# A hybrid encoder layer on one Trainium2 core: the input read with its channels first, the token's scale applied to the products

## The chip, the cores and the metric

The kernel runs on one core of a Trainium2 chip. The metric is the device time of one execution in microseconds (us). The engines are TensorE (PE in the profile; PEld is its weight load), VectorE (DVE), ScalarE (ACT), GpSimd (POOL) and SyncE (SP), which here issues nearly all DMA. Each engine works through its own instructions in order; semaphores tie the engines together.

## The reference, cut to what matters

One layer over two independent sequences (512 and 1024 tokens, laid behind each other: 1536 tokens, 1024 channels, all float32):

```python
u = x * rsqrt(mean(x*x, -1) + EPS) * g_norm            # EPS = 1e-6
z = u @ w_in                                           # 1024 -> 3072 columns
q, k, v, g_att, xr, g_lru = split(z, 512 columns each)
o_att = diff_attention(rms_norm(q), rms_norm(k), v)    # q, k normed per 32 columns
o_lru = rg_lru(conv4(xr))   # gates sigmoid(y @ w), two recurrences (forward, backward)
h = x + concat(o_att * silu(g_att), o_lru * silu(g_lru)) @ w_out
y = h + rms_norm((p @ w_ple) * sigmoid(h @ w_pg)) * g_ple
```

The change touches `u`, `z` and what takes `z` out of PSUM.

## The kernel before

**Arithmetic.** Every large product is done in three matmuls: each operand is split into a high part (fp32r) and the rest (`hi`, `lo`), and PE adds hi\*hi, lo\*hi and hi\*lo. ACT makes each `hi` by a copy, DVE or POOL makes each `lo` by a subtraction.

**The start (tokens to `u`).** For each of 12 tiles of 128 tokens: SP loads the tile `x_sb` (`load_x`, L470), ACT sums its squares (`square_x`, L1017), POOL makes the scale 1/sqrt (`x_scale`: L844, then a power, L846), DVE multiplies by scale and gain (`normalise`, L1349), PE turns it in 8 transposes (`transpose_u`, L1731), ACT splits off `u_hi` from PSUM (`split_u`, L1022) and DVE makes `u_lo` (`u_low`, L1354). The gain `g_norm` is spread over the partitions by 8 transposes first (L1773, L1341).

**The z blocks.** The 12 blocks of 128 columns of xr, g_lru and g_att (`m` = 0 to 11) times 3 blocks of 512 tokens (`b`) are 36 z blocks. The list `ZB` gives their order; a block's place in it is its number i, from 0. `z_block(i)` is 24 matmuls (L1721 to L1723) into one of three PSUM banks `b_ps[i % 3]`, so block i waits until block i - 3 has left PSUM (`z_evac`). The weights of a block come from `load_wA` (L475), `wA_high` (ACT, L1029) and `wA_low` (POOL, L854).
An xr block leaves PSUM by a DVE copy into XP (L1364). A gate block leaves it in two steps: `z_sigmoid` on ACT (L1059, PSUM to `z_stage`), then a DVE product of it with the PSUM bank (L1368), which frees the bank; SP stores it (`store_z`). The blocks of tiles 4 to 11 are turned between the matmuls of z blocks 0 to 3.

**The recurrence among the z blocks.** A loop over c = 0, 1, 2 does nine z blocks each, from number r = 9c + 8, and among them one group of 128 recurrence channels (channel group 3 follows among the q, k and v products). On PE: the six small gate products `gate(6c)` to `gate(6c+5)`, `gates = {0: (0, 1), 1: (2,), 3: (3, 4), 4: (5,)}`: gates 0 and 1 ahead of block r, 2 ahead of r+1, 3 and 4 ahead of r+3, 5 ahead of r+4 (numbers modulo 6). Gate g waits for `sig_done` g - 1, the ACT sigmoids of gates 0 to g - 2. Gate 6c waits for the convolution's result Y (`conv_taps`, DVE) and for its copy with swapped halves (`swap_rows`, a DMA). On ACT and DVE, in the order of the code (a part):

```python
# ACT                               # DVE
z_sigmoid(r)                        z_out_of_psum(r)
sig(g + 2)                          z_out_of_psum(r + 1)
z_sigmoid(r + 1)                    root_argument(c, 0)   # L1447
decays(c, 0)  # L1071, 1074, 1077   scan(c, 0)            # L1455, L1461
root(c, 0)    # L1081               z_out_of_psum(r + 2), (r + 3), (r + 4)
z_sigmoid(r + 2)                    conv_taps(c + 1, (0, 1, 2))
sig(g + 3)    # L1047, L1048        root_argument(c, 1)
```

**After it.** 36 products of q, k and v by tokens (L1817 to L1819), then 96 attention steps and the output products.

Of the kernel before, what the change touches and what calls it, by code (L numbers as in the profile page):

```python
# [30 lines left out]
P = 128  # L31
# [39 lines left out]
def encoder_layer(nc, x, p_in, g_norm, w_in, norms, lams, rel_bias, onehot, chan, w_a, w_x,  # L71
# [19 lines left out]
    with ctx:  # L91
# [11 lines left out]
        chan_sb = sb("chan_sb", [P, LC, 11])  # L103
        rate = sb("rate", [P, LC, 2])
# [3 lines left out]
        sums = sb("sums", [P, 5, 2])  # L108
        rsum = sb("rsum", [P, 24, 2])
# [3 lines left out]
        u_hi = sb("u_hi", [P, KC, T], F32R, phase1)  # L113
        u_lo = sb("u_lo", [P, KC, T], F32R, phase1)
        z_stage = sb("z_stage", [P, NB, 512], F32, phase1)
        sq_junk = z_stage
        wB_hi = [sb("wB_hi", [P, KC, 512], F32R, phase1)]
# [10 lines left out]
        wA_hi = sb("wA_hi", [P, 3, KC, P], F32R, phase1)  # L128
# [4 lines left out]
        ssq = sb("ssq", [P, 2, 16], F32, phase1)  # L133
        msq = sb("msq", [P, 2, 16], F32, phase1)
        rsq = sb("rsq", [P, 2, 16], F32, phase1)
        ph1a = ExitStack()
        x_sb = sb("x_sb", [P, 4, D], F32, ph1a)
        u_tok = sb("u_tok", [P, 2, D], F32, ph1a)
        gnB = sb("gnB", [P, D], F32, ph1a)
        x_junk = sb("x_junk", [P, D], F32, ph1a)  # L140
        ssx = sb("ssx", [P, 4], F32, ph1a)
        msx = sb("msx", [P, 4], F32, ph1a)
        rsx = sb("rsx", [P, 4], F32, ph1a)
# [91 lines left out]
        def k_tile(u, hh):  # L235
# [62 lines left out]
        const_in = sem("const_in"); gnB_in = sem("gnB_in"); gn_turned = sem("gn_turned"); soft_step = sem("soft_step")  # L298
# [4 lines left out]
        x_sq = sem("x_sq"); x_ms = sem("x_ms"); x_rs = sem("x_rs"); u_done = sem("u_done")  # L303
        uT_done = sem("uT_done"); uhi_done = sem("uhi_done"); ulo_done = sem("ulo_done")
# [35 lines left out]
            "g_in", "mixed", "hp_in0", "hp_in1", "x_sum", "m_hi", "m_lo", "p_in", "p_hi", "p_lo", "x_in", "gp_in",  # L340
# [43 lines left out]
        def uT_slot(n):  # L384
            if n == 2:
                return b_ps[:, 1:3, :].rearrange("p a b -> p (a b)")
            return (uT_ps[:, 0:2, :].rearrange("p a b -> p (a b)") if n == 0 or n % 2 and n > 1 else
                    qT_ps[:].rearrange("p a b c -> p (a b c)"))

        ZB = [(0, 0), (1, 0), (0, 1), (1, 1), (0, 2), (2, 0), (1, 2), (2, 1), (2, 2)]  # L390
        ZB += [(m, b) for m in range(3, 3 * LC) for b in range(NB)]
        LASTM = 3 * (LC - 1) + 1
        XR = (0, 2, 5, 8)

        def z_row(m):
            return m + 1 if m == LASTM + 1 else m
# [64 lines left out]
        def _(sp):  # L461
# [5 lines left out]
            def load_x(n):  # L467
                if n >= 4:
                    sp.wait_ge(u_done, n - 3)
                sp.dma_start(x_sb[:, n % 4, :], x[n * P:(n + 1) * P, :]).then_inc(x_in[n % 4], 16)  # L470

            def load_wA(m):
                if m >= 3:
                    sp.wait_ge(z_mm, z_blocks_to(m - 3))
                sp.dma_start(wA_raw[:, m % 3, :, :],  # L475
                             w_in.rearrange("(k p) c -> p k c", p=P)[:, :, 3 * A + m * P:3 * A + (m + 1) * P]
                             ).then_inc(wA_in[m % 3], 16)

            load_x(0)
            load_x(1)  # L480
            load_x(2)
            load_x(3)
            load_wA(0)
            load_x(4)
            load_x(5)
            load_wA(1)
            load_x(6)
            load_x(7)
# [7 lines left out]
            load_x(8)  # L496
            load_x(9)
            load_wA(2)
            load_x(10)
            load_x(11)  # L500

            def store_z(i):
# [4 lines left out]
                sp.wait_ge(z_evac, i + 1)  # L507
# [18 lines left out]
            def load_gate(c):  # L526
                if c:
                    sp.wait_ge(lru_out, 64 * c)
                for slot, stored in z_stored(gate_row(c)):
                    sp.wait_ge(z_out[slot], stored)  # L530
                row = z_row(gate_row(c)) * P
                sp.dma_start(G_[:, 0:LONG], z_ch[row:row + P, TOK0:T]).then_inc(lru_g_in, 16)
                sp.dma_start(G_[:, YS:YS + SHORT], z_ch[row:row + P, 0:TOK0]).then_inc(lru_g_in, 16)
# [15 lines left out]
            store_z(0)  # L549
            store_z(1)  # L550
            store_z(2)
            store_z(3)
            load_wA(3)
            store_z(4)
            sp.wait_ge(lru_clear, 1)
            load_gate_w(0)
            sp.wait_ge(line_sb, 4)
            sp.dma_start(line_d, line_st[:]).then_inc(line_out, 16)
            swap_rows(0)
            store_z(6)  # L560
            load_wA(4)
            store_z(7)
# [229 lines left out]
            for k in range(PC):  # L792
# [7 lines left out]
                         ).then_inc(fin["gp_in"], 16)  # L800
# [33 lines left out]
        def _(gp):  # L834
# [13 lines left out]
            def x_scale(n):  # L848
                rsqrt(n, ssx[:, n % 4:n % 4 + 1], msx[:, n % 4:n % 4 + 1], rsx[:, n % 4:n % 4 + 1], 1, D,
                      x_sq, x_ms, x_rs)  # L850

            def wA_low(m):
                gp.wait_ge(wAhi_done, m + 1)
                gp.tensor_tensor(wA_lo[:, m % 3, :, :], wA_raw[:, m % 3, :, :], wA_hi[:, m % 3, :, :].bitcast(F32),  # L854
# [14 lines left out]
            for n in range(NT):  # L869
                x_scale(n)  # L870
                if n == 3:
                    wA_low(0)
                if n == 5:
                    wA_low(1)
                if n == 11:
                    wA_low(2)
# [15 lines left out]
            step(gp.tensor_scalar(spv[2], spv[1], 1.0 / 17, 1.0 / 15, ALU.mult, ALU.add))  # L892
# [1180 lines left out]
```

## Time and profile before

| | us |
|---|---|
| median of 3 runs (1056.28 to 1058.12) | 1057.22 |
| the profiled execution | 1057.25 |
| its span | 1055.4 |
| PE busy | 1015.6 (96%) |
| DVE busy | 650.1 (62%) |
| ACT busy | 579.8 (55%) |
| POOL busy | 517.9 (49%) |

1.85 us of the profiled execution lie outside its span. PE is busy in nearly all of it; of 40 slices of 26.4 us the first is the one in which PE is busy for half only.

### The profile page before, as it was taken

The numbers are of one execution on the slowest core, as the hardware profiler recorded it, in microseconds if no ns is written. First come the engines' busy times: TensorE is split into PE (matmuls) and PEld (weight loads), VectorE is DVE, ScalarE is ACT, GpSimd is POOL, SyncE is SP. The second block draws the span as 40 slices with busy tenths as digits, with TensorE's granted clock in tenths as the row PEclk, the third lists the DMA queues.
The fourth block names the chain that finished last, engine by engine and source line by source line (L and its number), as shares of the span: only waits on it lengthen the run. The fifth ranks groups of instructions, "written<-read, shape, count | busy, mean of one in ns | idle before, by whom it ended". The sixth has DMA issues, their size and how long they took to land.

```text
span 1055.4 us, 15541 instructions
## 1 busy us (share of the span) xinstructions
PE 1015.6 (96%) x5856; PEld 806.3 (76%) x5856; DVE 650.1 (62%) x1026; ACT 579.8 (55%) x879; POOL 517.9 (49%) x421
## 2 busy tenths in 40 slices
PE   5999999999999999988999999999999999999997
PEld 4777877677787888866777777777778888888885
DVE  6743636574576251149999999999966355445423
ACT  6536567583653131159999999999962212112112
POOL 5252234526467542016666776766668143444421
PEclk8999999999999999999999999999999999999999
DMA  7231634323254624929876577364185222432221
GB/s 239 84 99 60 204 120 125 121 77 127 61 160 140 179 80 140 284 94 227 206 178 171 147 178 205 94 163 136 53 298 186 82 91 85 131 124 85 96 89 40
DMA packets 114810, 144.06 MB, mean 136 GB/s; under 512 B 10024, under 2 KB 80808, under 8 KB 114728
## 3 DMA queue, kind: packets, MB, share of 16 engines
q1 hardware_dynamic: 114592, 143.06, 45.6%
q8 instruction: 47, 0.77, 0.3%
q14 instruction: 27, 0.22, 0.1%
q10 hardware_dynamic: 144, 0.00, 0.0%
HBM read 95.78 MB, written 44.11 MB: 133 GB/s over the span
## 4 chain that ended last, share of the span: by engine, by line
PE 67%; DVE 18%; issue 10%; ACT 4%; DMA 1%; POOL 0%; DVEq 0%; POOLq 0%; SPq 0%; ACTq 0%
DVE E_ L1545 11%; PE b_ps L1721 5%; PE b_ps L1722 5%; PE b_ps L1723 5%; PE b_ps L1817 5%; PE b_ps L1819 5%; PE b_ps L1818 5%; PE g_ps L1721 4%; PE g_ps L1723 4%; PE g_ps L1722 4%; PE o_ps L1878 3%; PE w_ps L1861 2%; PE h_ps L1721 2%; PE h_ps L1723 2%; PE h_ps L1722 2%
## 5 line engine op out<-in xcount | busy, mean ns | idle before, releaser
L1188 ACT ACTIVATE E_<-E_,nmax 128x1024 f32<-128x1024 f32 (+1 forms) x184 | 186.7, 1017 | 15.0 <-DVE nmax L1545 14.7
L1545 DVE CUSTOM_DVE_ANT_0 E_<-s_ps,bias 128x1024 f32<-128x1024 f32 (+1 forms) x184 | 188.0, 1056 | 3.6 <-PE s_ps L1830 3.6
L930 POOL TENSOR_TENSOR E_<-E_,ratio 128x576 f32<-128x576 f32 (+3 forms) x92 | 84.7, 920 | 85.5 <-DVE E_ L1561 85.5
L1721 PE MATMUL b_ps<-u_hi,wA_hi 128*128 128x512 f32 x288 | 115.5, 401 | 5.3 <-DVE u_lo L1354 4.9
L1722 PE MATMUL b_ps<-u_lo,wA_hi 128*128 128x512 f32 x288 | 113.0, 392 | 0.0
L1723 PE MATMUL b_ps<-u_hi,wA_lo 128*128 128x512 f32 x288 | 112.9, 392 | 0.0
L933 POOL TENSOR_TENSOR E_<-E_ 128x576 f32<-128x576 f32 (+3 forms) x92 | 103.8, 1128 | 7.2
L1830 PE MATMUL s_ps<-KL,QL 128*128 128x512 f32 x256 | 90.3, 434 | 14.0 <-DVE nmax L1545 13.2
L1861 PE MATMUL w_ps<-ident,E_ 128*128 128x128 f32 x624 | 83.5, 273 | 1.8 <-ACT WT L1216 1.7
L1216 ACT ACTIVATE WT<-w_ps 128x1024 f32<-128x1024 f32 (+1 forms) x96 | 83.4, 868 | 2.8 <-PE w_ps L1861 2.6
L1878 PE MATMUL o_ps<-WT,V 128*64 128x128 f32 x1280 | 84.0, 278 | 0.0
L1861 PEld LDWEIGHTS w_ps<-ident,E_ 128*128 128x128 f32 x624 | 72.6, 141 | 14.8 <-issue 3.9
L1878 PEld LDWEIGHTS o_ps<-WT,V 128*64 128x64 f32 x1280 | 68.6, 136 | 18.8 <-issue 18.8
L1817 PE MATMUL b_ps<-wB_hi,u_hi 128*128 128x512 f32 x192 | 76.0, 396 | 0.5 <-DVE z_stage L1368 0.5
L1721 PEld LDWEIGHTS b_ps<-u_hi,wA_hi 128*128 128x128 f32 x288 | 54.4, 189 | 28.4 <-issue 17.7
L1721 PE MATMUL g_ps<-wg_hi,h_hi 128*128 128x512 f32 x192 | 75.6, 394 | 0.0
L1819 PE MATMUL b_ps<-wB_hi,u_lo 128*128 128x512 f32 x192 | 74.9, 390 | 0.0
L1723 PE MATMUL g_ps<-wg_hi,h_lo 128*128 128x512 f32 x192 | 74.8, 390 | 0.0
L1722 PE MATMUL g_ps<-wg_lo,h_hi 128*128 128x512 f32 x192 | 74.8, 389 | 0.0
L1818 PE MATMUL b_ps<-wB_lo,u_hi 128*128 128x512 f32 x192 | 74.7, 389 | 0.0
L854 POOL TENSOR_TENSOR wA_lo<-wA_raw,wA_hi 128x1024 fp32r<-128x1024 f32 x12 | 30.1, 2504 | 88.8 <-ACT wA_hi L1029 88.6
L846 POOL TENSOR_TENSOR rsq<-msq,neghalf 128x16 f32<-128x16 f32 x24 | 70.5, 2939 | 2.0
(226 smaller groups left out, 2338.5 us busy)
## 6 DMA issues: line engine op xcount, KB each, us to landing
QL<-qk_t SPq DMA_DIRECT2D x32, 256.0 KB, 6.3
KL<-qk_t SPq DMA_DIRECT2D x32, 256.0 KB, 7.7
bias<-line_d SPq DMA_DIRECT2D x8, 960.0 KB, 11.2
x_sb<-in_x SPq DMA_DIRECT2D x12, 512.0 KB, 5.0
wA_raw<-in_w_in SPq DMA_DIRECT2D x12, 512.0 KB, 4.1
z_ch<-z_stage SPq DMA_DIRECT2D x24, 256.0 KB, 2.0
qk_t<-qh SPq DMA_DIRECT2D x24, 256.0 KB, 2.3
qk_t<-ql SPq DMA_DIRECT2D x24, 256.0 KB, 2.8
```

The costliest lines, as they stand in the source:

```text
L933: gp.tensor_tensor(one, one, two, ALU.add).then_inc(w_gp, 1)
L1188: act.activation(e, e, ACT.Exp, bias=nmax[:, n % 5, c:c + 1], scale=-1.0, accum_out=sums[:, n % 5, c:c + 1]).then_inc(e_done, 1)
L1545: dve.tensor_tensor_reduce(weights_at(n)[:, c, 0:n_tok], s_ps[:, c, 0:n_tok], b[:, ::-1], -1.0, 3e38, ALU.add, ALU.min, nmax[:, n % 5, c:c ...
L1721: pe.matmul(dst, sh, mh, start=k == 0, stop=False)
L1722: pe.matmul(dst, sh, ml, start=False, stop=False)
L1723: mm = pe.matmul(dst, sl, mh, start=False, stop=k == n - 1)
L1817: pe.matmul(dst, u_hi[:, k, c], wB_hi[g][:, k, :], start=k == 0, stop=False)
L1818: pe.matmul(dst, u_hi[:, k, c], wB_lo[g][:, k, :], start=False, stop=False)
L1819: mm = pe.matmul(dst, u_lo[:, k, c], wB_hi[g][:, k, :], start=False, stop=k == KC - 1)
L1830: mm = pe.matmul(s_ps[:, c, b * 512:(b + 1) * 512], q_tile(u, hh)[:, c, qt * P:(qt + 1) * P], k_tile(u, hh)[:, c, b * 512:(b + 1) * 512], ...
L1861: mm = pe.transpose(w_ps[:, k, :], weights_at(n)[:, 0, k * P:(k + 1) * P], ident[:])
L1878: mm = pe.matmul(o_ps[HV * j:HV * j + HV, 0, pair * P:(pair + 1) * P], V_at[i % 2][:, first // P + k, HV * (head % 2):HV * (head % 2) + HV ...
```

## The change

The host passes the tokens a second time with the channels first (`x_t`), and the columns of the z blocks as 12 contiguous blocks (`w_cols`). `u` is now x times the gain only: ACT makes `u_hi` from the loaded `u_raw` with the gain as its scale, DVE makes `u_lo`; nothing is transposed for it. The scale of a token is still made from `x_sb`, four tiles at a time; PE spreads it over the partitions (`spread_row`, four transposes for 512 tokens), DVE copies it into `row`, and DVE multiplies each z block by it on its way out of PSUM (`z_scale`). The sigmoid of a gate block then reads the scaled `z_stage` and writes the PSUM bank `z_gate()`, and a second DVE product (`z_gated`) makes the result. q and k go unscaled (their own norm removes the factor; its EPS is scaled by `epsx`), v is scaled by the ACT copy that takes it out of PSUM. ZB, the loop's order (`LATE`) and the buffers of the weights change with it.

```diff
-        ZB = [(0, 0), (1, 0), (0, 1), (1, 1), (0, 2), (2, 0), (1, 2), (2, 1), (2, 2)]
+        ZB = [(0, 0), (1, 0), (2, 0), (0, 1), (1, 1), (0, 2), (2, 1), (1, 2), (2, 2)]
-        XR = (0, 2, 5, 8)
+        XR = (0, 3, 5, 8)
+        LATE = (2, 1, 0)
 # SP
+            load_xT(0, 0)
+            sp.dma_start(wA_raw[:, 0, 0:KC // 2, :], w_cols[0, :, 0:KC // 2, :]).then_inc(wA_half_in, 16)
+            sp.dma_start(wA_raw[:, 0, KC // 2:KC, :], w_cols[0, :, KC // 2:KC, :]).then_inc(wA_in[0], 16)
+            load_xT(0, 1)
             load_wA(1)
+            load_xT(0, 2)
+            load_xT(0, 3)
+            load_wA(2)
+            for n in range(4):
+                load_x(n)
+            sp.wait_ge(uhi_done, KC)
+            for j in range(KC // 2):
+                load_xT(1, j)
 # POOL
+            wA_low(0)
+            wA_low(1)
+            wA_low(2)
+            for b in range(NB):
+                x_scale(b)
 # ACT
+                act.activation(u_hi[:, b, k, :], u_raw[:, b, k, :], ACT.Copy, scale=g_col[:, k:k + 1]
+                               ).then_inc(uhi_done, 1)
...
+            wA_high(2)
             for n in range(4):
                 square_x(n)
+            for k in range(KC):
+                u_high(1, k)
+            z_sigmoid(1)
+            z_sigmoid(2)
+            for n in range(4, 8):
+                square_x(n)
+            for k in range(KC):
+                u_high(2, k)
+            z_sigmoid(4)
+            for n in range(8, NT):
+                square_x(n)
...
             def z_sigmoid(i):
-                act.wait_ge(z_mm, i + 1)
-                act.activation(z_stage[:, n % NB, :], b_ps[:, i % NB, :], ACT.Sigmoid).then_inc(z_sig, 1)
+                act.wait_ge(z_evac, i + 1)
+                act.wait_ge(z_fin, n)
+                act.activation(z_gate(), z_stage[:, n % NB, :], ACT.Sigmoid).then_inc(z_sig, 1)
...
+                def z_sigmoids(first, last):
+                    for i in range(first, min(last, 9)):
+                        z_sigmoid(r + i)
+                        if i == 3:
+                            wA_high(3 * c + 5)
+                        if i == 6 and c < LC - 2:
+                            wA_high(3 * c + 6)
...
-                z_sigmoid(r + 1)
+                z_sigmoids(late + 1, late + 2)
                 decays(c, 0)
                 root(c, 0)
-                z_sigmoid(r + 2)
+                z_sigmoids(late + 2, late + 3)
                 sig(g + 3)
 # DVE
+                dve.scalar_tensor_tensor(out=u_lo[:, b, k, :], in0=u_raw[:, b, k, :], scalar=g_col[:, k:k + 1],
+                                         in1=u_hi[:, b, k, :].bitcast(F32), op0=ALU.mult, op1=ALU.subtract
+                                         ).then_inc(ulo_done, 1)
...
+                    dve.tensor_tensor(z_stage[:, n % NB, :], b_ps[:, i % NB, :], tokens, ALU.mult
                                       ).then_inc(z_evac, 1)
+            def z_gated(i):
+                dve.wait_ge(z_sig, z_sigs(i))
+                dve.tensor_tensor(z_stage[:, n % NB, :], z_stage[:, n % NB, :], z_gate(), ALU.mult).then_inc(z_fin, 1)
+            def z_out_of_psum(i):
+                z_scale(i)
+                z_gated(i - 1)
...
+            row_out(0)
+            z_scale(0)
+            z_scale(1)
+            for k in range(KC):
+                u_low(1, k)
+            z_gated(1)
+            z_scale(2)
+            z_gated(2)
...
+                z_blocks(0, late + 2)
                 root_argument(c, 0)
                 scan(c, 0)
-                for i in range(2, 5):
-                    z_out_of_psum(r + i)
+                z_blocks(late + 2, late + 5)
 # PE
+            keep_busy(12)
+            z_block(0)
+            z_block(1)
+            z_block(2, lambda k: spread_row(0) if k == 4 else None)
+            z_block(3)
+            z_block(4, lambda k: spread_row(1) if k == 5 else None)
+            z_block(5)
+            z_block(6, lambda k: spread_row(2) if k == 5 else None)
+            z_block(7)
...
+                gates = {late: (0, 1), late + 1: (2,), late + 3: (3, 4), late + 4: (5,)}
```

`keep_busy(12)` is 12 transposes of the identity. `z_blocks(a, b)` is `z_out_of_psum` for r + a to r + b - 1. `spread_row(b)` waits for the scales of block b, which need the squares of its four tiles. Where a list says `LATE[c]`, all of channel group c's steps sit `late` blocks later among the z blocks than before.

## Rows read from the trace of the kernel before

**Rows 1.** Page, parts 1 and 2, busy time and slices:

```profile
PE 1015.6 (96%) x5856; PEld 806.3 (76%) x5856; DVE 650.1 (62%) x1026; ACT 579.8 (55%) x879; POOL 517.9 (49%) x421
PE   5999999999999999988999999999999999999997
```

**Rows 2.** Windows; after each engine's name its busy us, then granted clock, DMA share, GB/s:

```profile
0.00:20.00 20.00, 9.09 (x41) 7.31 (x42) 11.29 (x10) 14.44 (x20) 11.15 (x21) 0.93 0.85 278
75.00:252.00 177.00, 176.48 (x843) 130.31 (x841) 96.55 (x73) 115.25 (x122) 68.78 (x21) 1.00 0.35 110
```

**Rows 3.** Timeline of PE, start: start, duration, instruction, idle before it and releaser:

```profile
19.85 0.77 PE L1721 MATMUL b_ps<-u_hi,wA_hi 128*128 128x512 f32 x1 [4.32 <-DVE u_lo L1354]
20.84 0.63 PE L1723 MATMUL b_ps<-u_hi,wA_lo 128*128 128x512 f32 x1
21.27 0.63 PE L1721 MATMUL b_ps<-u_hi,wA_hi 128*128 128x512 f32 x1
```

**Rows 4.** Windows of the start, columns as in Rows 2:

```profile
6.00:7.00 1.00, 0.00 (x0) 0.00 (x0) 0.24 (x1) 1.00 (x2) 0.56 (x1) 1.00 1.06 434
7.00:8.00 1.00, 0.00 (x0) 0.00 (x0) 1.00 (x1) 0.82 (x2) 0.87 (x1) 1.00 0.96 380
20.00:22.00 2.00, 2.00 (x5) 1.62 (x6) 2.00 (x1) 0.43 (x2) 1.92 (x2) 0.50 0.09 26
```

**Rows 5.** Timeline of ACT: the first square, and a split:

```profile
4.57 1.06 ACT L1017 ACTIVATE x_junk<-x_sb 128x1024 f32<-128x1024 f32 x1 [2.09 <-DMA x_sb<-in_x]
5.89 1.06 ACT L1017 ACTIVATE x_junk<-x_sb 128x1024 f32<-128x1024 f32 x1 [0.17 <-DMA x_sb<-in_x]
13.03 1.05 ACT L1029 ACTIVATE wA_hi<-wA_raw 128x1024 fp32r<-128x1024 f32 x1
```

**Rows 6.** Timeline of DVE and of POOL between 14 and 24 us:

```profile
14.29 1.22 DVE L1354 TENSOR_TENSOR u_lo<-qT_ps,u_hi 128x1024 fp32r<-128x1024 f32 x1
19.62 4.50 DVE L1349 SCALAR_TENSOR_TENSOR u_tok<-x_sb,rsx,gnB 128x1024 f32<-128x1024 f32 x2
14.15 2.45 POOL L854 TENSOR_TENSOR wA_lo<-wA_raw,wA_hi 128x1024 fp32r<-128x1024 f32 x1 [1.42 <-ACT wA_hi L1029]
19.47 2.37 POOL L854 TENSOR_TENSOR wA_lo<-wA_raw,wA_hi 128x1024 fp32r<-128x1024 f32 x1 [1.01 <-ACT wA_hi L1029]
```

**Rows 7.** Timeline of PE in loop c = 0: gates 0, 3, 5 and the starts of blocks 9, 11:

```profile
75.50 0.64 PE L1765 MATMUL uT_ps<-Y,gate_w 64*64 64x512 f32 x1
84.06 0.50 PE L1721 MATMUL b_ps<-u_hi,wA_hi 128*128 128x512 f32 x1
95.19 0.64 PE L1765 MATMUL uT_ps<-Y,gate_w 64*64 64x512 f32 x1
97.07 0.50 PE L1721 MATMUL b_ps<-u_hi,wA_hi 128*128 128x512 f32 x1
102.84 0.64 PE L1765 MATMUL uT_ps<-Y,gate_w 64*64 64x512 f32 x1
```

**Rows 8.** Timeline of ACT and of DVE in loop c = 0:

```profile
89.86 0.60 ACT L1059 ACTIVATE z_stage<-b_ps 128x512 f32<-128x512 f32 x1 [4.39 <-PE b_ps L1723]
98.23 1.49 ACT L1081 ACTIVATE TH<-TH 128x1539 f32<-128x1539 f32 x1 [0.53 <-DVE TH L1447]
101.04 0.60 ACT L1059 ACTIVATE z_stage<-b_ps 128x512 f32<-128x512 f32 x1
102.10 0.69 ACT L1048 ACTIVATE I_<-qT_ps,chan_sb 128x512 f32<-128x512 f32 x1
104.84 1.27 DVE L1368 TENSOR_TENSOR z_stage<-z_stage,b_ps 128x512 f32<-128x512 f32 x2
```

**Rows 9.** Timeline of DVE and of SP around the swap of c = 1, and the copy's DMA line:

```profile
117.95 1.82 DVE L1431 SCALAR_TENSOR_TENSOR Y<-XP,chan_sb,Y 128x1539 f32<-128x1539 f32 x1
120.84 1.14 SPq L524 DMA_DIRECT2D Ysw<-Y  x2
Ysw<-Y SPq DMA_DIRECT2D x8, 384.8 KB, 4.4
```

## What the change was predicted to do

> **What bounds the kernel now.** I read the page's first two parts first. PE is busy for 96% of the span, and the slices show one weak place, the first, where it is half idle [rows 1]. The windows sharpen this: 9.1 of the first 20.0 us, but 176.5 of the 177.0 us between 75 and 252 us [rows 2]. So PE bounds the z blocks, and time is to be had ahead of them. The timeline of PE shows how: the first z matmul starts at 19.85 us, after an idle of 4.32 us [rows 3].
>
> A busy bound is not the only one. The timeline of loop c = 0 shows block 11 starting at 97.07 and gate 5 at 102.84 [rows 7]: 5.77 us for a block. Two blocks from 84.06 to 95.19 take 11.13 us [rows 7], so I count 5.46 a block (and 0.1 or 0.2 where a gate follows). Gate 5 starts just as ACT ends what it waits for: the sigmoid L1048 runs from 102.10 to 102.79 [rows 8]. So a second chain (sigmoid of block 9, decays, root, sigmoid of block 10, `sig(3)`, gate 5) runs beside PE with no slack. That is where a later hand-over shows.
>
> **The start.** Block 8 and the gates ahead of it come at 75.50 us before [rows 7]; I work out the same point after.
> - Landing. The first 512 KB tile is there at 4.57 us [rows 5], and then 434 and 380 GB/s flow [rows 4], about 1.3 us for 512 KB. In SP's new order the pieces of block 0 land at 4.6, 7.2, 9.8 and 11.1, the halves of the first weights at 5.2 and 5.9, wA 1 and 2 at 8.5 and 12.4, the four x tiles from 13.7 to 17.6.
> - The splits. A 1024-column copy on ACT takes 1.05 [rows 5], so 512 columns 0.55; a DVE operation on 512 columns 0.65 (two in 1.27 [rows 8]). `u_high(0, 0)` 4.6 to 5.2, `u_low` 5.8, the first `wA_lo` half 6.5: the first z matmul at 6.6, 13.3 us earlier than before [rows 3].
> - The lock. `u_low` took its input from PSUM and ran in 1.22 us beside POOL's `wA_lo` [rows 6]. Now it reads two SBUF operands, as `normalise` does, and two of those at 19.62 took 4.50 us together where POOL held `wA_lo` from 19.47 to 21.84 [rows 6]; free of it they would take about 2.4, as `u_low` twice. So such an operation waits POOL's whole 2.4 us. `wA_low(1)` (9.7 to 12.1) holds up `u_low(0, 4)`, `wA_low(2)` (13.9 to 16.3) holds up `u_low(0, 7)`. Block 0 then ends at 17.65, without the lock at 13.5. I take 17.65, and keep 4.1 us as the bound.
> - Blocks 1 and 2 to 29.1 with `spread_row`. `u_low(1, k)` stands behind `row_out(0)` and two `z_scale`, and goes on in step with PE (0.65 each against 0.69 for three matmuls): block 3 from 29.1 to 34.7.
> - Block 4 stops at its k = 5, 38.1, for `spread_row(1)`. That needs the squares of tiles 4 to 7, which stand on ACT behind `z_sigmoid(2)`, thus behind `z_scale(2)`, thus behind all of `u_low(1, k)`: 33.4, `z_gated(1)` 34.0, `z_scale(2)` 34.6, the sigmoid 35.3, four squares at 1.32 each (4.57 to 5.89 [rows 5]) 40.6, POOL's scale 42.1. A stop of 4.0 us; block 4 ends at 44.65, block 5 at 50.1.
> - Block 6 stops likewise at its k = 5 for tiles 8 to 11, whose squares stand behind `z_sigmoid(4)`: 53.5 to 55.4. It ends at 57.9, block 7 at 63.4, `lines` at 64.4.
>
> Block 8 is reached at 64.4 instead of 75.5: 11.1 us saved. With the lock's 4.1 back, 15.2 at most; with a slow PE after the stops, 9.
>
> A rule of the Trainium skill bears on this (SBUF — State Buffer, "SBUF: two separate sides"): a DVE operation with two SBUF inputs and a GpSimd one take the pair of ports as an exclusive lock for a whole instruction. The page names no such lock for an operation with one PSUM input. The trace agrees with both halves [rows 6]. Taken away, the rule would put my sum at 4.1 us less; by the 358 GB/s that the Trainium skill gives for a core's HBM reads (DMA: Bandwidth & Descriptors, "Specifications") block 0 would land 0.9 us later. Against that figure stand 434 and 380 GB/s here [rows 4], and the measurement decides.
>
> **The loops c = 0 to 2.** I count from the end of block r + late + 1, the last whose sigmoid stands ahead of `decays(c, 0)`. Before, that is block 9, whose sigmoid starts at 89.86; the root ends at 99.72, DVE's scan at 104.84, ACT's next sigmoid starts at 101.04, gate 5 at 102.84 [rows 8, 7].
> - In front of the sigmoid now stand `z_scale` (0.7) and, in c = 1, `z_gated(18)` (0.6), since `z_sigmoid` waits for both.
> - After the root `z_sigmoid(r + late + 2)` no longer reads PSUM. It waits for `z_scale` of the same block, which stands on DVE behind the scan, until 104.84 on the old scale instead of 101.04, then 0.65 for the scale and 0.6 for a `z_gated`. The sigmoid starts 5.1 us later; `sig(g + 3)` is queued behind it, and gate 5 of the group, and with it PE, behind that.
> - In c = 1 the step i = 3 falls there too, and `wA_high(8)` (0.95) goes in front of `sig(9)`.
> - Sums. c = 1: 0.7 + 0.6 + 5.1 + 1.0 = 7.4 us. c = 2 (block 26 is xr, the weight step lies behind): 0.7 + 5.1 = 5.8. c = 0: blocks 9 to 11 are xr, so `decays` starts right after `sig(2)`, which gives back nearly all: 0.6.
>
> Together 13.8 us of new stops of PE, where before there was none to speak of. Bounds: 11 (if DVE's small steps overlap better) and 16.
> - The copy for gate 6 and 12. Y was done at 119.77, its swap issued by 121.98 and landed 4.4 later [rows 9], five us before PE came. The blocks between `decays(c, 1)` and that gate fall from four to three, 5.46 less, and `z_scale`, `z_gated` and `wA_high(6)` lengthen the way: 1.5 and 1.6 us of stop, 3.1 together (0 to 5).
> - The clock. After 4.32 us idle PE ran at half rate: start to start 0.43 us [rows 3], clock 0.50 [rows 4], against 0.23 later (5.46 over 24); nine matmuls so before it rose, 1.8 us. The stops of 7.4 and 5.8 are longer than that idle: 3.6 us, 0 to 5.4 with the one of 4.0 at the start.
> - 24 more DVE products of 0.69 beside 96.6 busy of 177 [rows 2] cost nothing as work; without that room they would be 16 us. ACT and POOL do no more than before. Attention and the output are the same code, and PE is on their path, so the shift reaches the end.
>
> **Sum**, against the profiled execution (1057.25; span 1055.4 and 1.85 around it; the median is 1057.22): 1057.25 - 11.1 + 13.8 + 3.1 + 3.6 = 1066.65. I say 1066.5.
>
> **Rivals.**
> 1. Faster: the hand-over through `z_scale` stays off the path, and the start pays. Mechanism: PE reaches the fifth gate late enough, or DVE gets the scale out before the scan. Then only 0.7 three times is added: 1057.25 - 11.1 + 2.1 = 1048, and 1044 without the lock. It decides where the new stops of the loops stay under 11.1 us together. For it: DVE is half idle [rows 2]. Against: both queues are in order, and gate 5 had no slack [rows 7, 8].
> 2. Gains and losses cancel: lock gone (-15.2), stops at their lower bound (11 + 2), clock kept: 1055 to 1059.
> 3. The start gains nothing, as its loads have doubled and all stops run at the low clock: 1057.25 - 7 + 16 + 5 + 5.4 = 1077.
> 4. The change doesn't do what it says: the scale's own chain (x tiles, squares, spread) is still ahead of the first blocks' exit, so that z would wait as before: the stops of 4.0 and 1.9 us are this, and no more, unless the banks fill earlier.
>
> **Numbers.** The forecast's case has 0.60, with its own range 1061 to 1073; rival 1 has 0.27, rival 2 0.08 (half of it within 0.2%, a quarter to each side), rival 3 (with 4) 0.05. About 0.2%, 2 us, is what a measurement can tell from no change. Faster 0.29, same 0.04, slower 0.67. The range for 8 in 10 takes in the upper part of rival 1: 1048 to 1073.
>
> **What would show it.** First z matmul near 6.6 us. PE idle of about 4 us inside block 4. POOL's `wA_lo` beside a stretched `u_lo`. The gates ahead of block 8's neighbours: block 8 starting near 64. Idle of 7 and 6 us ahead of the sixth gate in c = 1 and c = 2, ended by the ACT sigmoid, the ACT queue waiting for DVE's `z_scale` after the scan, and clock 0.50 after them. Wrong it would be if PE runs densely from 64 us on: then the time is near 1048.

## The result, and the profile after

| | before | after |
|---|---|---|
| median (4 runs each, on one chip) | 1057.53 (1056.28 to 1058.12) | 1083.4 (1082.54 to 1085.43) |
| the profiled execution | 1057.25 | 1083.45 |
| its span | 1055.4 | 1081.6 |
| PE's granted clock, mean over the span | 0.995 | 0.983 |

The changed kernel is slower: after / before = 1.0249, with a 95% interval of 1.0231 to 1.0267. The forecast was 1066.5 with a range of 1048 to 1073. So the direction was right, the time lies 10 us above the range, and 16.9 us of the size are missing.

The page after, parts 1 and 2 (busy time and slices), answers to [rows 1]:

```profile
PE 1015.1 (94%) x5776; PEld 801.7 (74%) x5776; DVE 653.8 (60%) x1053; ACT 583.1 (54%) x891; POOL 511.7 (47%) x406
PE   6899988779999999997999999999999999999997
PEclk9999998889999999999999999999999999999999
```

PE's busy time is as before, though it does 80 matmuls less. The first slice is a little better, 6 for 5, the second a little worse, 8 for 9. Then slices 6 to 9 (27.0 us each, so 135 to 243 us) show 8, 8, 7, 7 where before there were nines, and from slice 7 to 9 the granted clock falls. Two windows, answering to [rows 2], put numbers on it:

```profile
0.00:20.00 20.00, 11.48 (x39) 8.66 (x39) 10.71 (x9) 13.96 (x20) 7.40 (x10) 1.00 0.90 334
75.00:252.00 177.00, 151.84 (x690) 109.23 (x689) 86.47 (x72) 97.16 (x102) 58.94 (x18) 0.92 0.30 97
```

Between 75 and 252 us PE did 690 matmuls where it had done 843, at a mean clock of 0.92. All other engines did less in it too: nobody was overloaded, all of them waited. So the loss is one of order, and the timeline of PE names each wait. Here are the start and the idle times up to gate 20 (two of the start's small ones left out); start, duration, instruction, in brackets the idle before it and its releaser. It answers to [rows 3, 7]:

```profile
8.83 0.77 PE L1805 MATMUL b_ps<-u_hi,wA_hi 128*128 128x512 f32 x1 [4.45 <-DVE wA_lo L1450]
18.04 0.50 PE L1805 MATMUL b_ps<-u_hi,wA_hi 128*128 128x512 f32 x1 [1.83 <-DVE u_lo L1410]
43.72 0.94 PE L1813 MATMUL uT_ps<-ident,rsx 128*128 128x128 f32 x4 [3.42 <-POOL rsx L888]
66.16 0.50 PE L1805 MATMUL b_ps<-u_hi,wA_first_hi 128*128 128x512 f32 x1
105.10 0.64 PE L1859 MATMUL uT_ps<-Y,gate_w 64*64 64x512 f32 x1 [0.53 <-ACT I_ L1094]
130.26 0.61 PE L1859 MATMUL uT_ps<-Y,gate_w 64*64 64x512 f32 x1 [2.08 <-DMA Ysw<-Y]
166.40 1.11 PE L1859 MATMUL uT_ps<-Y,gate_w 64*64 64x512 f32 x1 [8.82 <-ACT I_ L1094]
194.00 0.96 PE L1859 MATMUL uT_ps<-Y,gate_w 64*64 64x512 f32 x1 [2.72 <-DMA Ysw<-Y]
207.07 0.64 PE L1859 MATMUL uT_ps<-Y,gate_w 64*64 64x512 f32 x1 [3.78 <-ACT I_ L1094]
235.62 1.11 PE L1859 MATMUL uT_ps<-Y,gate_w 64*64 64x512 f32 x1 [7.23 <-ACT I_ L1094]
267.50 0.61 PE L1859 MATMUL uT_ps<-Y,gate_w 64*64 64x512 f32 x1 [0.40 <-DMA Ysw<-Y]
275.05 0.64 PE L1859 MATMUL uT_ps<-Y,gate_w 64*64 64x512 f32 x1
```

In order these are: the first z matmul; the last stop in block 0 (one of 0.69 us lies ahead of it); block 4 at its `spread_row(1)` (one of 0.19 us follows in block 6); block 8; then gates 5, 6, 11, 12, 14, 17, 18; and gate 20, which comes after the loops. The trace of before has gate 20 here:

```profile
250.52 0.64 PE L1765 MATMUL uT_ps<-Y,gate_w 64*64 64x512 f32 x1
```

**Where the 26.2 us of the span went.** I cut both traces at the same two places, gate 20 and block 8 (before with gates 0 and 1 ahead of it, which after stand ahead of block 10 and so behind this cut).
- Up to block 8: 66.16 for 75.50 [rows 7], -9.3.
- Block 8 to gate 20: 275.05 - 66.16 = 208.9, before 250.52 - 75.50 = 175.0: +33.9. The idle times of the fence between the two add up to 25.6, before they are some 0.3. What is left, 8.6, is slow running behind them: four windows below give 8.4 by the granted clock.
- Gate 20 to the end of the span: 806.55 for 804.88, +1.7. One idle time in the q products is 2.29 us here and 1.04 before, and behind it the clock was 0.50 from 354.6 to 358.0, which is 1.7 more; 1.2 us of these 3.0 come back ahead of the attention.

**The hand-over, hop by hop.** This is the sixth gate of c = 1 (gate 11, idle 8.82), on DVE:

```profile
144.63 0.69 DVE L1432 TENSOR_TENSOR z_stage<-b_ps,row 128x512 f32<-128x512 f32 x1 [6.01 <-PE b_ps L1807]
145.24 0.68 DVE L1441 TENSOR_TENSOR z_stage<-z_stage,qT_ps 128x512 f32<-128x512 f32 x1
157.71 3.36 DVE L1541 TENSOR_TENSOR_SCAN HF<-A_,I_ 128x1539 f32<-128x1539 f32 x1
160.99 0.67 DVE L1432 TENSOR_TENSOR z_stage<-b_ps,row 128x512 f32<-128x512 f32 x1
161.57 0.68 DVE L1441 TENSOR_TENSOR z_stage<-z_stage,qT_ps 128x512 f32<-128x512 f32 x1
```

and on ACT:

```profile
146.01 0.60 ACT L1104 ACTIVATE qT_ps<-z_stage 128x512 f32<-128x512 f32 x1 [5.54 <-DVE z_stage L1441]
154.38 1.49 ACT L1126 ACTIVATE TH<-TH 128x1539 f32<-128x1539 f32 x1 [0.53 <-DVE TH L1527]
162.32 1.28 ACT L1104 ACT_TABLE_LOAD   x1 [6.45 <-DVE z_stage L1441]
163.62 0.60 ACT L1104 ACTIVATE qT_ps<-z_stage 128x512 f32<-128x512 f32 x1
164.15 1.04 ACT L1075 ACTIVATE wA_hi<-wA_raw 128x1024 fp32r<-128x1024 f32 x1
165.67 0.68 ACT L1094 ACTIVATE I_<-qT_ps,chan_sb 128x512 f32<-128x512 f32 x1
```

Read it from the end. PE starts gate 11 at 166.40, when `sig(9)` (165.67) is done. In ACT's queue there stand ahead of it the copy `wA_high(8)`, the sigmoid of the next z block and the table load for it, and all that waits from 155.87 to 162.32. DVE has the product `z_gated` that releases it at 161.57 only, since `z_scale` of the same block (160.99) stands behind the scan (157.71, 3.36). The bank was full long before. Before the change the same sigmoid read PSUM itself and came 2.81 us after the start of the root [rows 8]; here it is 9.24 us.

One hop was not foreseen. Before, the table was loaded right behind the root: the root ended at 99.72 and the sigmoid ran at 101.04 [rows 8]. Here the load stands behind the wait for DVE, so its 1.28 us lie on the chain too. The load before:

```profile
99.74 1.28 ACT L1059 ACT_TABLE_LOAD   x1
```

### The profile page after: what moved, and what is told of

The parts are those of the page before. It is cut to its first block, busy times and chain, and to the rows that moved or that the text cites. A ratio compares the mean times of both kernels' runs of the same rounds, so it can differ in the third digit from the quotient of the medians.

```text
span 1081.6 us, 15433 instructions
## 1 busy us (share of the span) xinstructions
PE 1015.1 (94%) x5776; PEld 801.7 (74%) x5776; DVE 653.8 (60%) x1053; ACT 583.1 (54%) x891; POOL 511.7 (47%) x406
## 4 chain that ended last, share of the span: by engine, by line
PE 56%; DVE 22%; issue 12%; ACT 7%; DMA 2%; POOL 1%; SPq 0%; DVEq 0%; POOLq 0%; ACTq 0%
DVE E_ L1629 10%; PE b_ps L1908 5%; PE b_ps L1910 5%; PE b_ps L1909 5%; PE g_ps L1805 4%; PE g_ps L1807 4%; PE g_ps L1806 4%; PE b_ps L1805 3%; PE b_ps L1807 2%; PE o_ps L1971 2%; PE b_ps L1806 2%; PE w_ps L1954 2%; PE s_ps L1921 2%; PE h_ps L1805 2%; PE h_ps L1807 2%
## 5 line engine op out<-in xcount | busy, mean ns | idle before, releaser
L1805 PE MATMUL b_ps<-u_hi,wA_hi 128*128 128x512 f32 x240 | 99.0, 412 | 7.1 <-DVE wA_lo L1450 4.4
L1921 PE MATMUL s_ps<-KL,QL 128*128 128x512 f32 x256 | 90.8, 436 | 13.8 <-DVE nmax L1629 13.0
L1806 PE MATMUL b_ps<-u_lo,wA_hi 128*128 128x512 f32 x240 | 96.2, 401 | 0.0
L1954 PEld LDWEIGHTS w_ps<-ident,E_ 128*128 128x128 f32 x624 | 72.6, 140 | 14.9 <-issue 3.8
L896 POOL TENSOR_TENSOR wA_lo<-wA_raw,wA_hi 128x1024 fp32r<-128x1024 f32 (+1 forms) x10 | 26.9, 2694 | 91.5 <-ACT wA_hi L1075 91.5
L1805 PEld LDWEIGHTS b_ps<-u_hi,wA_hi 128*128 128x128 f32 x240 | 47.1, 196 | 29.9 <-issue 10.5
## 6 DMA issues: line engine op xcount, KB each, us to landing
bias<-line_d SPq DMA_DIRECT2D x8, 960.0 KB, 11.1
```

The source lines that it names most:

```text
L1805: pe.matmul(dst, sh, mh, start=k == 0, stop=False)
L1806: pe.matmul(dst, sh, ml, start=False, stop=False)
L1921: mm = pe.matmul(s_ps[:, c, b * 512:(b + 1) * 512], q_tile(u, hh)[:, c, qt * P:(qt + 1) * P], k_tile(u, hh)[:, c, b * 512:(b + 1) * 512], ...
L1954: mm = pe.transpose(w_ps[:, k, :], weights_at(n)[:, 0, k * P:(k + 1) * P], ident[:])
```

## Experiments

All times are medians; each ratio is against the kernel before, run on the same chip. All edits are made to the changed kernel, except where another is named. The last four columns are idle times of PE in us, ahead of the gate or in the block named.

| kernel | us | ratio (95% interval) | block 4 | gate 11 | gate 14 | gate 17 |
|---|---|---|---|---|---|---|
| after | 1083.4 | 1.0249 (1.0231 to 1.0267) | 3.42 | 8.82 | 3.78 | 7.23 |
| e1_scale_first | 1068.53 | 1.0114 (1.0099 to 1.0129) | 3.42 | 2.40 | 3.78 | 0.80 |
| e2_weights_behind_sig | 1079.38 | 1.0213 (1.0197 to 1.0228) | 3.42 | 8.82 | none | 7.23 |
| e3_squares_first | 1078.17 | 1.0203 (1.0188 to 1.0218) | none | 8.82 | 3.78 | 7.23 |
| e10_swap_first | 1081.27 | 1.0219 (1.0200 to 1.0239) | 3.46 | 8.82 | 3.78 | 7.23 |
| e7_lock_at_start | 1080.85 | 1.0228 (1.0214 to 1.0241) | 3.43 | 8.83 | 3.78 | 7.23 |
| e8_pe_kept_busy | 1083.32 | 1.0246 (1.0233 to 1.0260) | 3.47 | 2.27 | 3.78 | 0.67 |
| e4_all_four | 1058.51 | 1.0013 (1.0003 to 1.0022) | none | 2.40 | none | 4.43 |
| e5_table_early | 1057.64 | 1.0008 (0.9999 to 1.0017) | none | 2.40 | none | 4.43 |
| e6_root_and_sigs_early | 1049.43 | 0.9932 (0.9918 to 0.9945) | none | 0.93 | none | 0.66 |
| e9_best | 1048.09 | 0.9917 (0.9902 to 0.9932) | none | 0.93 | none | 0.62 |

The kernel before took 1056.9 to 1057.1 beside these runs. Executions of one of these kernels differ by up to 5.5 us (e6: 1047.50 to 1052.99). One thing that differs from trace to trace, at places where the code is the same, is where PE ran at clock 0.50 (the last section lists it). So gains of 2 us are read from the traces as well.

**e1: the scale of one block ahead of the scan.**

```diff
                 root_argument(c, 0)
+                z_blocks(late + 2, late + 3)
                 scan(c, 0)
-                z_blocks(late + 2, late + 5)
+                z_blocks(late + 3, late + 5)
```

> DVE does z_out_of_psum(r + late + 2) between root_argument(c, 0) and scan(c, 0) instead of behind the scan; nothing else differs from the changed kernel (1083.4 us). Theory (queue order): the ACT sigmoid, and with it sig(g + 3) and the sixth gate, waited for a product that DVE had room for 5.1 us earlier. Then the idle of PE ahead of the sixth gate falls from 8.8 to 3.7 us in c = 1 and from 7.2 to 2.1 in c = 2, the 0.5 in c = 0 goes, and with less low clock the time is 1067 to 1071. Rival (capacity): DVE or ACT has too much work in these stretches, so that the idle only moves; it stays above 6 us in both and the time above 1080.

1068.53, 14.9 us less than after. DVE's product is now at 156.93, the table load at 158.56 and the scan at 160.38; gate 11 waits 2.40 and gate 17 0.80:

```profile
157.05 1.49 ACT L1126 ACTIVATE TH<-TH 128x1539 f32<-128x1539 f32 x1 [0.53 <-DVE TH L1527]
156.93 0.68 DVE L1432 TENSOR_TENSOR z_stage<-b_ps,row 128x512 f32<-128x512 f32 x1
160.38 3.36 DVE L1541 TENSOR_TENSOR_SCAN HF<-A_,I_ 128x1539 f32<-128x1539 f32 x1
```

The scan was not put off by it: it starts 3.33 us behind the root (157.05, in after 154.38) in both, because DVE had stood idle there for 1.56 us, waiting for the root. The two waits fell 1.3 us lower than I expected (3.7 and 2.1), since the table load now runs right behind the root. This is the main cause, shown: one place in DVE's order. The idle removed is 13.4 us (0.53, 6.42, 6.43), and 1.0 comes back at gate 18 (1.41 for 0.40); the rest of the gain is less slow running, clock 0.96 for 0.92 between 75 and 252 us.

**e2: the weights' copy behind the group's first sigmoid.**

```diff
-                wA_high(3 * c + 4)
                 z_sigmoids(0, late)
                 sig(g)
+                wA_high(3 * c + 4)
                 sig(g + 1)
```

> ACT does wA_high(3c + 4) between sig(g) and sig(g + 1), as before the change, instead of ahead of sig(g). Theory: the 3.8 us idle ahead of gate 14 is a wait of this split for the last z block of its buffer (two buffers where there were three), with sig(12) queued behind it; it goes, with 1.7 us of low clock behind it: 1077 to 1079. Rival: gate 14 is late because the swapped copy came late and everything on ACT with it; then the idle stays over 3 us and the time at 1083.

1079.38, 4.0 us less (its executions: 1077.63 to 1081.06). Gate 14's 3.78 is gone, the other waits stand. On ACT after (the kernel as changed), the wait is this:

```profile
203.39 1.06 ACT L1075 ACTIVATE wA_hi<-wA_raw 128x1024 fp32r<-128x1024 f32 x1 [8.08 <-PE b_ps L1807]
204.46 1.28 ACT L1093 ACT_TABLE_LOAD   x1
206.34 0.68 ACT L1094 ACTIVATE I_<-uT_ps,chan_sb 128x512 f32<-128x512 f32 x1
```

`wA_high(10)` writes one of two buffers, which only the last matmul of block 26 frees. It waits 8.08 us for it, with the table load and `sig(12)` queued behind, and gate 14 waits for `sig(12)`. The copy itself isn't wanted for three blocks yet.

**e3: the squares ahead of the sigmoids.**

```diff
-            z_sigmoid(1)
-            z_sigmoid(2)
             for n in range(4, 8):
                 square_x(n)
+            z_sigmoid(1)
+            z_sigmoid(2)
             for k in range(KC):
                 u_high(2, k)
-            z_sigmoid(4)
             for n in range(8, NT):
                 square_x(n)
+            z_sigmoid(4)
```

> ACT does the squares of tiles 4 to 7 ahead of z_sigmoid(1) and z_sigmoid(2), and those of 8 to 11 ahead of z_sigmoid(4). Theory: the 3.4 us idle of PE inside block 4 is the scale's chain queued behind a sigmoid that waits for DVE; it goes, and 1.7 us of low clock behind it, and the shift reaches the end: 1078 (1077 to 1080). Rival (given back): the loops' stops are set by chains that do not start earlier when PE does, and take up the gain: 1082 to 1084.

1078.17, 5.2 us less, for a stop of 3.42. Behind the stop PE had run slowly, and now it doesn't. First after, then e3, the window behind block 4's stop (columns as in Rows 2; the number before the DMA share is the clock):

```profile
44.00:47.00 3.00, 3.00 (x10) 2.45 (x9) 2.96 (x6) 3.00 (x6) 0.43 (x1) 0.50 0.81 314
```

```profile
44.00:47.00 3.00, 3.00 (x15) 2.49 (x14) 3.00 (x5) 1.81 (x3) 0.00 (x0) 1.00 1.02 408
```

Ten matmuls in three microseconds against fifteen: some 1.7 us of the 5.2 fits this. It isn't a price of its own, though: e1's execution had the same stop of 3.42 with clock 1.00 behind it, and there block 6 waited 1.82 instead of 0.19, so that block 8 came equally far behind the stop (22.46 us for 22.44). What e3 takes away is the chain of the squares.

**e10: the swap ahead of a store in SP's queue.**

```diff
-                store_z(r + 5)
                 swap_rows(c + 1)
+                store_z(r + 5)
```

> The changed kernel (1083.4 us) with swap_rows(c + 1) issued ahead of store_z(r + 5), nothing else. Theory: in c = 1 SP waits for z_gated(22) ahead of the swap, 1.3 us behind the convolution's last tap; the idle ahead of gate 12 falls from 2.7 to about 1.3 us, that ahead of gate 6 stays near 2.1: 1081.5 to 1083. Rival: the idle is the DMA's own landing (4.4 us) and stays 2.7: 1083.4.

1081.27, 2.1 us less; the two intervals overlap a little, so the time alone doesn't show it. After (the kernel as changed), SP issued them so:

```profile
187.69 0.33 SPq L533 DMA_DIRECT2D z_ch<-z_stage  x1
188.11 1.15 SPq L549 DMA_DIRECT2D Ysw<-Y  x2
```

Y was done at 186.47 (184.65 and 1.82). The store ahead of the swap waited for its block's `z_gated`, which the change had put behind a `z_scale`. Before, the swap stood behind a store too, 1.07 us behind Y [rows 9]; here it is 1.64. With the swap first, gate 12 waits 0.95 instead of 2.72, and from gate 11 to gate 14 it takes 37.2 us for 40.7: the 1.8 of idle and 1.7 of slow running behind it. Against that, e10's execution had a slow stretch behind gate 6 that after's had not. Gate 6's own wait hardly changed (1.91 for 2.08): its swap had no wait ahead of it.

**e7: block 0's third `wA_lo` on DVE instead of POOL.**

```diff
 # POOL
-            wA_low(2)
 # DVE, behind u_low(0, 7)
+            dve.wait_ge(wAhi_done, 4)
+            dve.wait_ge(wAlo_done, 3)
+            dve.tensor_tensor(wA_lo[:, 2, :, :], wA_raw[:, 2, :, :], wA_high_at(2).bitcast(F32),
+                              ALU.subtract).then_inc(wAlo_done, 1)
```

> The changed kernel (1083.4 us) with wA_low(2) done by DVE behind u_low(0, 7) instead of by POOL beside it; POOL keeps wA_low(0) and wA_low(1). Theory (lock): the 1.8 us idle of PE in block 0 is u_low(0, 7) held up by POOL's wA_lo; it goes, and u_lo of 512 columns takes 0.75 us throughout the second half of block 0. Time 1081 to 1082. Rival (landing): k = 6 and 7 come late by DMA or by the ACT copies, and the idle stays above 1.2 us; time 1083.

1080.85, 2.5 us less, with intervals that just overlap. Block 0's last stop (1.83) is gone, and block 1 starts at 17.29 for 19.53. The same four `u_low` in after, with POOL's operation at that time, and then in e7:

```profile
12.11 6.54 DVE L1410 SCALAR_TENSOR_TENSOR u_lo<-u_raw,g_col,u_hi 128x512 fp32r<-128x512 f32 x4 [0.41 <-ACT u_hi L1062]
15.06 2.38 POOL L896 TENSOR_TENSOR wA_lo<-wA_raw,wA_first_hi 128x1024 fp32r<-128x1024 f32 x1 [1.11 <-ACT wA_first_hi L1075]
```

```profile
12.24 4.09 DVE L1409 SCALAR_TENSOR_TENSOR u_lo<-u_raw,g_col,u_hi 128x512 fp32r<-128x512 f32 x4 [0.70 <-ACT u_hi L1061]
```

The difference, 2.45, matches POOL's 2.38. So the rival, landing, is out for this stop.

**e8: PE kept busy through the waits.** In c = 1 and 2, 60 transposes of the identity ahead of the sixth gate; they write a z bank that is free.

```diff
                 for i in range(9):
+                    if c and i == late + 4:
+                        pe.wait_ge(z_evac, r + i - NB + 1)
+                        for _ in range(60):
+                            pe.transpose(b_ps[:, (r + i) % NB, 0:P], ident[:], ident[:])
```

> The changed kernel with 60 transposes of the identity on PE (into a PSUM bank about to be overwritten) ahead of the sixth gates of c = 1 and c = 2, 6.5 us of the idle 8.8 and 7.2. No wait is taken away. Theory: half rate behind these two stops costs half of the busy time at 0.50, (170.3 - 166.4)/2 + (242.0 - 235.6)/2 = 5.2 us; with PE busy the clock stays up and they come back: 1078 (1077 to 1079.5). Rival: the low clock is hidden, since the stops that follow are set by ACT and DVE chains and not by PE: 1082 to 1084.

1083.32, no different from after: the expected 5 us didn't come. What the clock does behind gate 17 is as expected, first in after, then in e8:

```profile
237.60:242.00 4.40, 4.40 (x12) 3.45 (x12) 0.00 (x0) 1.74 (x3) 3.74 (x2) 0.51 0.00 0
```

```profile
237.70:242.00 4.30, 4.30 (x23) 2.92 (x24) 0.00 (x0) 3.67 (x6) 1.70 (x1) 1.00 0.16 61
```

and gate 17 to gate 18 took 28.9 us for 31.9. But in c = 1 the filling fell short by 2.27 us, and the clock fell behind it all the same. And behind gate 6, where the edit does nothing, the clock was 1.00 in after's execution and 0.54 in this one, with nearly the same idle ahead of it (2.08 and 2.16). First after, then e8:

```profile
130.30:134.20 3.90, 3.90 (x25) 2.25 (x26) 3.83 (x3) 1.56 (x2) 0.44 (x1) 1.00 0.96 314
```

```profile
130.80:134.20 3.40, 3.40 (x16) 0.85 (x16) 3.33 (x3) 1.25 (x2) 0.13 (x1) 0.54 0.96 345
```

The places of the gates say where the expected 5.2 went. Gate 11 comes 2.2 us later than in after, 1.7 of it by the slow stretch behind gate 6. Behind gate 11 nearly as much ran slow as before. The 3.0 us behind gate 17 did come back: gate 18 is 0.9 us earlier than in after. So slow running does cost time on PE's path, and this run's equal time is, in the profiled execution, 3.0 us won against some 2 lost; what it was in the other executions isn't known.

**e4: edits 1, 2, 3 and 10 together.**

> The three edits together, and SP issues swap_rows(c + 1) ahead of store_z(r + 5), which waits for z_gated. Theory: the edits add, since each takes away a stop of its own (10.7 + 3.8 + 3.4 us), the swap's order gives 1 to 2, and the low clock (some 12 us of half rate, half of it lost work) goes nearly wholly; left over are waits of about 4 us ahead of the sixth gates and 1 to 3 ahead of gates 6 and 12: 1051 (1047 to 1057), faster than the kernel before. Rival (capacity of ACT and DVE between two groups of channels, whose distance fell from nine z blocks to eight): the stops reappear elsewhere and the time stays above 1062.

1058.51: the four gains, 14.9 + 4.0 + 5.2 + 2.1 = 26.2, would give 1057.2. They add up within 1.3 us, so they are four causes and not one seen four times, though a wait that grew is hidden in the sum. It is not the 1051 that I expected (at most 1057). What was left is mainly a wait of 4.43 at gate 17, where e1 alone had left 0.80:

```profile
182.93 8.45 POOL L907 TENSOR_TENSOR wB_lo<-wB_raw,wB_hi 128x1024 fp32r<-128x1024 f32 x2 [1.38 <-ACT wB_hi L1133]
193.03 3.84 DVE L1519 TENSOR_TENSOR G_<-HF,G_ 128x1539 f32<-128x1539 f32 x1
196.90 1.50 ACT L1171 ACTIVATE lru_hi<-G_ 128x1539 fp32r<-128x1539 f32 x1 [6.25 <-DVE G_ L1519]
212.45 1.11 PE L1860 MATMUL uT_ps<-Y,gate_w 64*64 64x512 f32 x1 [4.43 <-ACT I_ L1094]
```

DVE's last steps of group c = 1 run beside POOL's `wB_lo` and are stretched, ACT's copy `lru_hi` waits 6.25 us for them, and c = 2's chain behind it is late. Most of the stretch isn't new: the scan took 5.39 in after and 5.44 here. New are 2.1 us in `G_` (3.84 for 1.76), beside POOL's next `wA_lo`, and that PE, freed of gate 14's stop, reaches gate 17 sooner. That the stretch is the lock of e7 is read from their lying side by side; it was not tried by itself, and e6 shows that the wait goes without it.

**e5: e4 and the table load ahead of the waits.**

```diff
+            act.wait_ge(ident_done, 2)
+            act.activation(under_constants[:, 0:1], neghalf[:, 0:1], ACT.Copy)
             act.wait_ge(gain_in, 16)
```

> As the kernel with all four edits (1058.5 us), with one ACT copy of one column ahead of the wait for the gain and for the first tokens, so that ACT's first table load (1.28 us) runs while the tokens come. Theory: the first z matmul starts 1.3 us earlier (7.5 instead of 8.9), but block 0's end is set by the landing of its later pieces and by POOL's wA_lo, so only 0 to 1 us reaches the end: 1057.5 to 1058.5. Rival: the whole start is ACT's chain; 1.3 us or more come back: 1057 or less.

1057.64, 0.9 less than e4, with intervals that overlap. The first z matmul is at 7.46 for 8.83 of after, 1.4 earlier, but block 1 starts at 19.19 for e4's 19.68. So at most 0.5 us of it is kept, and block 0's end is set by something else. The load ran here at 1.20, ahead of the waits.

**e6: e5 and ACT's order changed twice.**

```diff
                 root(c, 0)
-                z_sigmoids(late + 2, late + 3)
                 sig(g + 3)
                 sig(g + 4)
+                z_sigmoids(late + 2, late + 3)
...
                 decays(c, 1)
-                z_sigmoids(late + 5, late + 6)
                 root(c, 1)
+                z_sigmoids(late + 5, late + 6)
```

> As e5_table_early, and on ACT root(c, 1) ahead of z_sigmoid(r + late + 5), and sig(g + 3), sig(g + 4) ahead of z_sigmoid(r + late + 2). Theory: what is left of the gate waits (2.4 us in c = 1, 4.4 in c = 2) is queue order too: in c = 1 the sigmoid and wA_high(8) stand ahead of sig(9) (1.5 us); in c = 2 the root of c = 1 waited 4.8 us behind a sigmoid for DVE, which made scan, sum and lru_high late. Idle under 1 us in c = 1 and under 2 in c = 2, clock full in the loops: 1049 to 1053, faster than the kernel before. Rival (capacity and the port lock: DVE's scan and sums stretched to 5.4, 3.3 and 3.8 us beside POOL's wB_lo): c = 2 keeps 3 us or more, and the time stays at 1055 or above.

1049.43, 8.2 less than e5 and 0.7% less than before (0.9932, at most 0.9945). What the gates need no longer stands behind what a z block needs. Gate 11 waits 0.93 for 2.40 and gate 17 0.66 for 4.43. The rival (capacity and the ports) is out: DVE's scan and sums are as long as in e4 (5.40, 3.32, and 3.85 for `G_`), only earlier. Which of the two moves did how much was not tried. The idle times between block 8 and gate 20 fell by 3.8 us only (9.7 to 5.9); the rest fits slow running, of which e5's trace has three stretches up to 331 us and e6's none. Windows, as the second of [rows 2]:

```profile
75.00:252.00 177.00, 171.11 (x812) 127.43 (x811) 108.17 (x89) 108.96 (x115) 76.92 (x24) 1.00 0.35 115
```

812 matmuls and a clock of 1.00, where after had 690 and 0.92.

**e9: e6 with e7's edit.**

> As e6_root_and_sigs_early (1049.4 us), with wA_low(2) on DVE as in e7_lock_at_start. Theory: the start's idle of 1.74 us in block 0 goes and, since PE is dense behind it but for waits that shift with it, reaches the end: 1047 (1046.5 to 1048.5). Rival: the waits ahead of gates 6 and 12, ended by a DMA, hang on DVE's convolution and not on PE, and take it up: 1049 to 1050.

1048.09, ratio 0.9917 (0.9902 to 0.9932). It is the fastest version here; against e6 it is 1.3 us, and the two intervals overlap, so that step alone isn't shown by the time. In the traces the start's stop is gone and block 1 starts 1.9 us earlier.

## Why the prediction was half right

The way was right. The step that failed is the sum of stops and slow running in the loops: forecast 13.8 + 3.1 + 3.6 = 20.5 us, measured 33.9 between block 8 and gate 20. Most of the gap comes from two terms. Gate 14 was put at nothing ("ACT and POOL do no more than before"), and was 3.8 us of idle. The clock was given two slow stretches, 3.6 us, and took 8.6 behind four. The rest is the table load in the hand-over (2.8) and the copy for gates 6 and 12 (2.1). The terms one by one:

- **The start: forecast -11.1, measured -9.3.** The steps were right: doubled loads, block 4's stop (forecast 4.0, measured 3.42), POOL's `wA_lo` beside a stretched `u_lo`. The first z matmul came at 8.83 and not at 6.6, since the tokens landed at 5.19, not 4.57, and the table load stood behind that wait. But that isn't the missing 1.8 us, as e5 shows. Block 0 ended at 19.53 for the forecast's 17.65, and the trace shows its third piece there at 11.3 and not at 9.8: between 5.2 and 11.36 us 367 GB/s flowed, where I had counted 1.3 us for 512 KB, some 400. The difference then stays (block 3 at 31.16 for 29.1, block 8 at 66.16 for 64.4).

```profile
5.19 1.28 ACT L1062 ACT_TABLE_LOAD   x1 [5.19 <-DMA u_raw<-in_x_t]
11.36 2.62 ACT L1062 ACTIVATE u_hi<-u_raw,g_col 128x512 fp32r<-128x512 f32 x4 [0.23 <-DMA u_raw<-in_x_t]
```

```profile
5.20:11.36 6.16, 2.53 (x6) 2.08 (x7) 3.84 (x5) 5.92 (x9) 1.69 (x2) 1.00 1.02 367
```

  Block 6's stop was 0.19 and not 1.9, but only because PE had run slowly ahead of it: in e1's execution, without that, it was 1.82. The rule on the ports held for the new form too: the Trainium skill (SBUF — State Buffer, "SBUF: two separate sides") has the lock last for the whole instruction, and the trace agrees (e7: 2.45 us for POOL's 2.38).
- **The sixth gates: forecast 13.8 (0.6, 7.4, 5.8), measured 16.6 (0.53, 8.82, 7.23).** This was the main step of the forecast, and it is right: place, queue, releaser, and e1 undid it. The two large terms are 1.4 us short each, and the table load's 1.28 is what the sum had left out; e1, which puts the load back behind the root, brings both waits 1.3 us below what I expected of it. I had taken the load to follow the root as in [rows 8], without asking on which side of the new wait it would stand.
- **The copy for gates 6 and 12: forecast 3.1, measured 4.8** (and 0.4 at gate 18). At gate 12 (1.6, measured 2.72) the missed part is SP's own order, shown by e10: the swap stood behind a store that waits for `z_gated`. I had counted the blocks between and not the queue. Gate 6 (1.5, measured 2.08) has no such store, and its 0.6 us stay unexplained.
- **Gate 14: forecast nothing, measured 3.8, and 1.7 of slow running behind it.** This step failed outright: "ACT and POOL do no more than before". ACT's work is the same, but its order had changed: `wA_high(3c + 4)` went ahead of `sig(g)`, and it waits for one of two buffers. The prediction followed the busy time of that copy and not what it waits for. e2 shows it.
- **The clock: forecast 3.6, measured some 12.** Of it 8.6 is the remainder in the loops, about 1.7 lies behind block 4's stop (where it delayed nothing of its own) and 1.7 in the q products. The forecast gave slow running to two stops, of nine matmuls each. In fact the clock fell behind each stop of the loops over 2.1 us. Windows of after from gates 11, 12, 14 and 17 on:

```profile
166.40:170.30 3.90, 3.90 (x13) 1.90 (x14) 0.00 (x0) 2.85 (x5) 1.72 (x2) 0.51 0.43 144
194.00:197.60 3.60, 3.60 (x17) 0.93 (x17) 3.56 (x2) 1.30 (x2) 3.17 (x2) 0.53 0.30 121
207.07:211.30 4.23, 4.23 (x15) 2.59 (x16) 0.00 (x0) 3.63 (x5) 3.04 (x2) 0.60 0.00 0
235.60:242.00 6.40, 6.38 (x19) 3.82 (x20) 0.00 (x0) 3.74 (x6) 3.74 (x2) 0.51 0.11 41
```

  Behind each of the four the clock stood at 0.50 (1.2 GHz; the windows also hold the first matmuls after it rose), and was back at 1.00 (2.4 GHz) within 3.5 to 6.5 us. The share of the clock that is missing, times the length, is 1.9, 1.7, 1.7 and 3.1 us. These add up to 8.4, worked out without the remainder of 8.6 and nearly the same. So the price was not in proportion to the stop: 1.7 behind 2.72 us, 1.9 behind 8.82.
- **The sum.** Forecast terms +9.4; measured: -9.3 (which holds block 4's slow stretch) + 25.6 - 0.3 + 8.6 + 1.7 = +26.3, against 26.2 in the spans. Of the 16.9 us missing, 1.8 are the start, 2.8 the sixth gates, 2.1 the swap, 3.8 gate 14, and 6.7 the clock (8.6 + 1.7 - 3.6, if all of the last stretch is given to it). That makes 17.2; before's own 0.3 us of idle bring it to 16.9.
- **The rivals.** Rival 1 (hand-over off the path, 1048) did not happen; its condition, DVE getting the scale out ahead of the scan, is e1's edit. With the rest mended the kernel reaches 1048.09, the number of that rival. That number is luck: e9 stands at -17.4 us at block 8 and +6.4 in the loops, the rival at -11.1 and +2.1. Rival 3 came nearest on the time (1077), but for the wrong reason: the start did gain. Of rival 4 no more came than the stops of 3.42 and 0.19. The range was too narrow since all its bounds were bounds on waits that I had found; none stood for a wait not found.

## What to carry to other kernels

When a step is given a second hop (here PSUM to DVE, then to ACT, instead of PSUM to ACT), write down for each in-order queue what stands ahead of the new hop and what stands behind the engine that waits for it; a 0.67 us product behind a 3.36 us scan cost 15 us, and moving one line gave them back. Do the same for each instruction that is merely moved: look at its wait (a buffer, a table, a store ahead of it), not at its duration. And give each stop of 2 us or more in a dense stream of matmuls a range of its own for the clock: here between nothing and 3.1 us on top.

## What was not expected of the hardware

- The table load of ACT waits with the instruction that it serves, where other waits stand ahead (1.28 us behind the landing at 5.19, and behind DVE's product at 162.32). A one-column operation ahead of the wait moves it out of the way (e5: first z matmul at 7.46 for 8.83).
- PE's clock fell from 2.4 to 1.2 GHz behind the idle times of 2.7 to 8.8 us among the z blocks of after. But length alone doesn't tell. Behind gate 6, with 1.91 to 2.21 us idle ahead of it in all traces since the change, it fell in e1, e8 and e10 and in no other. Behind block 4's stop of 3.42 us it was 0.50 in after and 1.00 in e1. Behind the 2.30 us in the q products it fell in e5 and not in e6. At the start too: before, the clock stood at 0.50 behind 4.32 us idle [rows 3, 4]; after, behind twelve transposes and 4.45 us idle, it stayed at 1.00, but in e7, e8 and e10, with the same code up to there and 4.2 to 4.3 us, it was 0.50. From e10:

```profile
8.60:11.50 2.90, 2.90 (x7) 2.32 (x8) 1.92 (x3) 2.29 (x3) 1.54 (x1) 0.50 1.03 418
```

  So a stop has no single price, the transposes didn't make sure of the clock, and the forecast's rule (longer than 4.32, so slow) was too simple in both directions.
